# One of two expert tables read by rows: 64 tokens in slots of partitions, summed by VectorE, beside a dense product that keeps all eight PSUM banks

## The reference, cut to what matters

```python
def peer(h, wq, sub_keys, u_tab, v_tab):          # u_tab, v_tab: 16384 x 1024 float32 each
    def one(hx):
        qq = (hx @ wq).reshape(pb, PEER_HEADS, 2, PEER_HALF)
        s = jnp.einsum('nhcd,hckd->nhck', qq, sub_keys)
        s1, i1 = lax.top_k(s[:, :, 0], PEER_TOPK)
        s2, i2 = lax.top_k(s[:, :, 1], PEER_TOPK)
        cand = s1[..., :, None] + s2[..., None, :]
        top, sel = lax.top_k(cand, PEER_TOPK)
        eidx = take(i1 * PEER_NKEYS + i2, sel)      # 128 rows per token
        g = jax.nn.softmax(top, axis=-1)
        a = jax.nn.gelu(jnp.einsum('nd,nhkd->nhk', hx, u_tab[eidx]))
        return jnp.einsum('nhk,nhkd->nd', g * a, v_tab[eidx])
```

## Time and profile before

| | |
|---|---|
| median of 3 runs | 1192.62 us |
| span of the profiled execution (first to last instruction) | 1199.7 us |
| U phase ends, first value tile starts | 827.93 us |
| last value tile starts | 1193.82 us |
| TensorE busy, share of the span | 97% |
| VectorE / ScalarE / POOL busy | 71% / 53% / 52% |
| DMA over the span | 268.42 MB, 224 GB/s in the mean |

### The profile page before, as it was taken

The page is one execution under the profiler, slowest core; times in us unless marked ns, Lnnn a source line. Parts: engine busy times, 40 slices in busy tenths (PEclk is TensorE's granted clock), DMA queues, the critical chain, the costliest instruction groups (busy, mean ns, idle before and its releaser), DMA issues.

```text
span 1199.7 us, 23707 instructions
## 1 busy us (share of the span) xinstructions
PE 1165.4 (97%) x8356; PEld 1087.5 (91%) x8356; DVE 850.4 (71%) x1594; ACT 632.0 (53%) x1207; POOL 623.4 (52%) x540
## 2 busy tenths in 40 slices
PE   7999999989999999999999999999989999999998
PEld 5698989977899999999999999999879888888888
DVE  6468456654686799999958788877756556656666
ACT  6454455432353454554557776745545555555554
POOL 2422234431000287877788877031477777777770
PEclk9999899899999999999999999999999999999999
DMA  7772439767664357677676666697988888888784
GB/s 246 273 235 74 141 104 336 232 196 255 195 238 171 105 186 174 169 169 188 172 186 168 157 169 169 222 328 258 335 288 300 285 291 298 304 294 297 284 293 168
DMA packets 143079, 268.42 MB, mean 224 GB/s; under 512 B 51504, under 2 KB 81776, under 8 KB 142256
## 3 DMA queue, kind: packets, MB, share of 16 engines
q1 hardware_dynamic: 101856, 208.60, 51.3%
q0 software_dynamic: 38384, 54.89, 17.5%
q10 hardware_dynamic: 2720, 3.40, 0.8%
HBM read 250.37 MB, written 20.62 MB: 226 GB/s over the span
## 4 chain that ended last, share of the span: by engine, by line
PE 86%; issue 4%; DVE 4%; ACT 2%; DMA 2%; POOLq 1%; another core or an unknown queue 1%; POOL 0%; SPq 0%; ACTq 0%; DVEq 0%
PE ps L2285 27%; PE ps L2365 15%; PE ps L2290 13%; PE ps L2372 8%; PE ps L2409 3%; PE ps L1831 2%; PE ps L1995 2%; PE ps L2098 2%; PE ps L1851 2%; PE ps L2136 1%; PE ps L1917 1%; PE ps L2103 1%; PE ps L2339 1%; PE ps L2086 1%; PE ps L1858 1%
## 5 line engine op out<-in xcount | busy, mean ns | idle before, releaser
L1044 ACT ACTIVATE w_hi<-ring 128x1024 fp32r<-128x1024 f32 x280 | 296.6, 1059 | 320.8 <-issue 189.2
L1541 DVE TENSOR_TENSOR w_lo<-ring,w_hi 128x1024 fp32r<-128x1024 f32 x271 | 331.2, 1223 | 181.7 <-ACT w_hi L1044 86.1
L2285 PE MATMUL ps<-h_hi,w_hi 128*128 128x288 f32 x1088 | 294.5, 299 | 0.5 <-ACT w_hi L1044 0.5
L2285 PE MATMUL ps<-h_lo,w_hi 128*128 128x288 f32 x1024 | 277.0, 295 | 0.0
L628 POOL DMA_INDIRECT gates<-arena x128 | 243.2, 1900 | 64.3 <-issue 43.7
L2285 PEld LDWEIGHTS ps<-h_hi,w_hi 128*128 128x128 f32 x1088 | 205.0, 188 | 1.2 <-ACT w_hi L1044 1.0
L638 POOL DMA_INDIRECT arena<-in_v,aux x122 | 148.5, 1217 | 90.3 <-DVE aux L1715 40.0
L2285 PEld LDWEIGHTS ps<-h_lo,w_hi 128*128 128x128 f32 x1024 | 192.2, 188 | 0.0
L2290 PE MATMUL ps<-h_hi,w_lo 128*128 128x288 f32 x1088 | 167.2, 296 | 0.2 <-DVE w_lo L1541 0.2
L2365 PE MATMUL ps<-h_hi,w_hi 128*128 128x432 f32 x680 | 149.8, 361 | 3.7 <-issue 1.8
L2290 PEld LDWEIGHTS ps<-h_hi,w_lo 128*128 128x128 f32 x1088 | 151.7, 188 | 0.5 <-DVE w_lo L1541 0.5
(11 more groups left out here) (375 smaller groups left out, 2041.5 us busy)
## 6 DMA issues: line engine op xcount, KB each, us to landing
ring<-in_uT SPq DMA_DIRECT2D x128, 512.0 KB
ring<-in_v SPq DMA_DIRECT2D x128, 512.0 KB
ring<-in_wout SPq DMA_DIRECT2D x32, 512.0 KB
ring<-in_wT SPq DMA_DIRECT2D x28, 512.0 KB
gates<-aux SPq DMA_DIRECT2D x32, 256.0 KB, 5.7
act_kept<-arena SPq DMA_DIRECT2D x32, 144.0 KB
ring<-in_wtok SPq DMA_DIRECT2D x8, 512.0 KB
aux<-gates SPq DMA_DIRECT2D x16, 256.0 KB
```

Source lines behind the costliest of these rows:

```text
L1044: act.activation(w_hi[e % 2][:, :], ring[:, (W_O + e) % RING, :], ACT.Copy).then_inc(S["w_high"], 1)
L1541: dve.tensor_tensor(w_lo[e % 2][:, :], ring[:, (W_O + e) % RING, :], w_hi[e % 2][:, :].bitcast(F32), ALU.subtract)\
L2285: last = pe.matmul(ps[:, bank, 0:NT], w_hi[e % 2][:, k * P:(k + 1) * P], mov[:, k, :], start=(k == 0 and mov is mov_hi), stop=False, skip_ ...
```

## The change

The tokens by rows become 64 (two sets x of 32), the dense ones 224; the groups of `route` become 24 (the last at tile 117, it was 113).

**Slots.** The 128 partitions hold 32 tokens x 4 pairs of heads. A pair of heads has 32 experts per token, so there are 32 slots; slot i of set x is one row of 1024 columns on every partition. POOL fetches it with two requests of 128 x 512. VectorE multiplies it by a weight per partition and adds it to a sum of 128 x 1024 per set (`weigh_slot`, one `scalar_tensor_tensor` per set). At the end TensorE adds the four partitions of a token and turns the sums in one product with a 128 x 32 matrix of ones and zeros (`turn_sums`, 8 matmuls for each half of the width), straight into columns 448 to 511 of the banks that hold the dense sums. Slots stand in the program at tiles 8, 12, 15, 19, 22, ... 120: five in 18 tiles. Each slot after the second is requested when tile 10, 13, 17, ... 114 is reached and slot i - 2 has been added, since two slots per set are held.

**Width.** The two halves of the width alternate from tile to tile, in eight banks (4 to 7 and 0 to 3), so a split moving side serves two tiles. The last four tiles are ordered half 0, 0, 1, 1.

**Lists.** The row numbers are now made for slots: ScalarE copies the picked indices into place at tile 68 of the U phase (5 small copies), VectorE computes the addresses right there (`gather_lists`, before after the last group, at tile 114), and TensorE no longer turns the indices of the 32 sample tokens (12 small matmuls). `act_kept` is written with the tiles of a partition side by side.

```diff
-NE = 72
+NE = 64
+QUADS = P // NS
+SLOTS = PTOP * PH // QUADS
+HELD = 2
+def row_tile(i):
+    return 10 + (i - HELD) * 18 // 5
+def slot_tile(i):
+    return row_tile(i + 1) + 2
-VBANK = ((2, 3, 4, 5), (0, 1, 2, 3))
+VBANK = ((4, 5, 6, 7), (0, 1, 2, 3))
+V_ORDER = [(t // 2, t % 2) for t in range(PK - 4)] + [(HALF - 2, 0), (HALF - 1, 0), (HALF - 2, 1), (HALF - 1, 1)]
...
 POOL:
+            def gather_rows(x, i):
+                n = NS * x + i
+                for half in range(2):
+                    pool.indirect_dma_start(e_rows[x][i % HELD][:, half * 512:(half + 1) * 512], None,
+                                            A["v"].rearrange("t p (c f) -> (t p c) f", f=512),
+                                            bass.IndirectOffsetOnAxis(row_list[:, n:n + 1], 0), element_offset=half * 32 * P * D)\
+                        .then_inc(S[row_sems[x][i % HELD]], 16)
+            for i in range(HELD, SLOTS):
+                pool.wait_ge(S["lo_used"], E_V + row_tile(i))
+                if i > FOUR and i % FOUR == HELD:
+                    pool.wait_ge(S["s_weights"], 2 + i // FOUR)
+                for k in range(2 * (i + FOUR - HELD), 2 * (i + FOUR - HELD) + 2):
+                    if k < 2 * SLOTS:
+                        gather_value(k)
+                for x in range(2):
+                    pool.wait_ge(S["rows_used"], 2 * (i - HELD) + x + 1)
+                    gather_rows(x, i)
...
 VectorE:
             copy_lists()
+            gather_lists()
...
+            def weigh_slot(i):
+                if i % FOUR == 0:
+                    dve.wait_ge(S[f"e_in{i // FOUR % 2}"], 16 * 2 * FOUR * (i // FOUR // 2 + 1))
+                    four = lambda y: y.rearrange("p (x n) -> p x n", x=2)[:, :, i:i + FOUR]
+                    dve.tensor_tensor(four(e_weights), four(e_act), four(gT[:, ND:NT]), ALU.mult).then_inc(S["s_weights"], 1)
+                dve.wait_ge(S["s_weights"], 2 + i // FOUR + 1)
+                for x in range(2):
+                    w = e_weights[:, NS * x + i:NS * x + i + 1]
+                    dve.wait_ge(S[row_sems[x][i % HELD]], row_base[x][i % HELD] + 32 * (i // HELD + 1))
+                    if i == 0:
+                        last = dve.tensor_scalar(e_sums[x], e_rows[x][0], w, None, ALU.mult)
+                    else:
+                        dve.wait_ge(S["rows_used"], 2 * (i - 1) + x + 1)
+                        last = dve.scalar_tensor_tensor(out=e_sums[x], in0=e_rows[x][i % HELD], scalar=w, in1=e_sums[x], op0=ALU.mult, op1=ALU.add)
+                    last.then_inc(S["rows_used"], 1)
             for t in range(2, PK):
                 w_low_part(E_V + t)
-                if t + 1 < PK:
-                    mov_low_part(t + 1)
+                if t % 2 == 0 and t // 2 + 1 < HALF:
+                    mov_low_part(t // 2 + 1)
                 if PK - WEIGH_AT + t - 2 < PIECES_IN:
                     weigh_piece(PK - WEIGH_AT + t - 2)
+                if t in SLOT_AT:
+                    weigh_slot(SLOT_AT[t])
...
 TensorE:
-                if t in UNIT_TILES:
-                    weigh_unit(2 * UNIT_TILES.index(t))
-                    weigh_unit(2 * UNIT_TILES.index(t) + 1)
-                if t == PK - 2:
-                    turn_sums()
                 value_tile(t)
+                if t in (SUM_AT, SUM_AT + 1):
+                    turn_sums(t - SUM_AT)
```

More of the change, by code:

```diff
@@ L221, in low_count @@
     return e + 1 - (POOL_LOW[1] - POOL_LOW[0] if e >= POOL_LOW[1] else 0)
[L224 to L231 removed]
+V_ORDER = [(t // 2, t % 2) for t in range(PK - 4)] + [(HALF - 2, 0), (HALF - 1, 0), (HALF - 2, 1), (HALF - 1, 1)]
 def v_tile(t):
[L235 removed]
+    pp, dh = V_ORDER[t]
     return pp // 32 * 64 + dh * 32 + pp % 32
@@ L642, in gather_value @@
[L642 to L659 removed]
+            row_list, act_list = (x[:, ND:NT].bitcast(U32) for x in (i1T, i2T))
@@ L1816, in _ @@
-            dve.wait_ge(S["x1_back"], 32)
-            dve.wait_ge(S["so_turned"], 3)
-            for dh in range(2):
-                x = xT[:, 4 * dh:4 * dh + 4, ND:NT].rearrange("p k (c q) -> p k c q", q=GRP)
-                new = ps[:, 6 + dh, :].rearrange("p (k q c) -> p k c q", k=4, q=GRP)[:, :, 0:EGROUPS, :]
-                last = dve.tensor_tensor(x, x, new, ALU.add)
-            last.then_inc(S["y_ready"], 1)
+                if t in SLOT_AT:
+                    weigh_slot(SLOT_AT[t])
@@ L1823, in _ @@
+            add_sums(0, range(4))
             add_sums(1, range(4))
@@ L2355, in value_tile @@
             def value_tile(t):
-                dh = t // HALF
+                pp, dh = V_ORDER[t]
                 e = E_V + t
-                both = [mov[t % MOVES][:, 2 * h * ND:2 * h * ND + 2 * ND] for h in range(2)]
+                both = [mov[pp % MOVES][:, 2 * h * ND:2 * h * ND + 2 * ND] for h in range(2)]
                 def high(ms):
```

250 lines of the change are left out of this document (88 added, 162 removed).

## The result

The changed kernel takes 1207.16 us (median of 5 runs, 1202.27 to 1211.84) against 1193.74 (5 runs, 1190.37 to 1197.34) for the kernel before: ratio 1.0116 [1.0087, 1.0145], slower by 1.2%. The forecast was 1177, with 1158 to 1203 as its range; the time lies above it.

What follows compares the result with a forecast made beforehand. TensorE bounded the kernel before; after the change POOL's requests would, at X = 10.2: V phase 48.9 + 29.3 X = 347.8 us, 18.1 less, U phase +2.8, span 1184.4, minus 7.1 for the median: 1177 us, range 1158 to 1203.

Steps and rivals of the forecast that it cites:

- What bounds the kernel: V phase before the change: 365.9 us, 2.45 us per value tile, 17 us of waits; POOL already at its limit.
- TensorE.: V phase for TensorE alone: 36.9 us removed, 9.8 added for columns, 1.0 for turning sums; 339.8 us with waits kept.
- 4.40: Microseconds, start to start, where TensorE weighed a group of 4 tokens before; the profile after should show none.
- U phase.: Two more groups add 1.3 us, the address list moved to tile 70 adds 1.5; together +2.8 us.
- VectorE.: A sum of 128 x 1024 takes 1.28 us; a slot needs 8.1 of 9.1 us, so it fits at 89%.
- second pass: Rival: a sum takes two passes on VectorE, 2.4 us; phase 386 us, median 1215; chance 0.03.
- X: POOL's time for the six requests of a slot: 10.2 us, between bounds of 9.1 and 11.3.
- But for one only: A POOL request waits for the running VectorE operation, but for no second one, then takes some 0.82 us more.
- POOL, the term that decides: POOL's requests set the V phase: 48.9 + 29.3 X, 347.8 us at X = 10.2, 18.1 less than before.
- Its chain: Late requests make rows late; VectorE waits ahead of the sum, TensorE for the next `w_lo`, SP to reload the ring.
- The landing of 4 us: Time for requested rows to arrive, 4 us, counted after POOL's requests at the end of the V phase.
- The slower rival: POOL's requests lock to VectorE's rhythm, six taking 10.65 us or more; median 1200 to 1209 us; chance 0.20.

Runs made afterwards that it cites:

- e2: Changed kernel with the 62 sums replaced by reductions with one SBUF input, leaving out the weighted sum: 1197.31 us, 0.9979 of the kernel before.
- e4: Changed kernel with one request per row of 1024 columns instead of two of 512: 1176.22 us, 0.9821 of the kernel before.
- e10: Changed kernel with only the gates two tiles earlier: 1195.12 us, 1.0123 of the kernel before.
- a2: The changed kernel as it is, measured again beside other runs on one chip: 1204.63 us, 1.0099 of the kernel before.
- e1b: Changed kernel with the value requests made four slots earlier, run beside the unedited change: 1187.27 us, 0.9948 of the kernel before.
- e5: Changed kernel with one request per row of 1024 columns and values requested four slots earlier: 1167.22 us, 0.9855 of the kernel before.
- e3: Changed kernel with values requested four slots earlier and reductions in place of the sums: 1183.35 us, 0.9879 of the kernel before.

## Why the prediction was wrong

By its own steps:

- *What bounds the kernel*: TensorE's tiles took 2.45 us and POOL ran near its limit; no run contradicts it.
- *TensorE.* A tile takes 2.51 us for 2.53. The turns lengthen two tiles to 4.23 and 4.32, together by 3.5 us where 1.8 was in the sum: each turn has 16 small matmuls (four blocks of columns for each of two sets), not 8 as the section on the change and the sum have it, and they take 1.72 us. No 4.40 is left.
- *U phase.* +2.8 (420.9 to 423.7), as forecast, with the gap at tile 70 where it was expected (the tile takes 2.2 us more, behind `w_lo`, for 1.5).
- *VectorE.* 1282 ns for 1.28 us; no second pass. `w_lo` is unchanged.
- *X, the time of six requests*: 10.14 us in the first trace, 9.7 on chip C, for 10.2. The mechanism (a sum holds a request) is shown by e2. "But for one only" is wrong: of 184 requests 87 were free, 88 waited for one operation, two for two (2.0 us), six for three (3.70 us each) and one for seven (6.64 us); before, 108 of 208 were free and 100 waited for one. Against a wait of one operation (some 1.4 us) the nine longer ones add about 20 us to the 184 requests, an estimate from these lengths, or 0.6 to X. That 10.2 was hit is so in part luck.
- **The step that failed is the phase's formula in "POOL, the term that decides"**: "28 slots x X and two with 4 requests instead of 6, i.e. 29.3 X". It holds only if POOL never stands still from tile 10 to the last slot. With the measured X it gives 48.9 + 29.3 x 10.14 = 346.0 us, the trace has 377.7. Of the missing 31.7 us, 23.6 are time in which POOL stands idle between its first gated request and its last (the 9.9 us at tile 10 come before that, inside the formula's 27 us, of which 26.2 were used). The other part is the end: behind POOL's last request the trace has 30.8 us, the formula 21.9. The last two slots have four requests each, POOL is ahead of the tiles again and waits 3.6 us for its last gate, and the rest is TensorE's own tiles. On chip C the terms are 25.6, 29.3 x 9.68, 34.0 of idle time and 30.7, together 373.9 as measured.

Why POOL idles is what the prediction didn't see. Its chain knew one wait of VectorE, for rows. The other stands in the diff: `weigh_slot` waits at every fourth slot for the values of four slots, and the last of these is asked for in the block of the slot after: behind the slot's own four row requests, and behind a gate that lies two tiles, 5 us, ahead of the use. Two requests take 2.2 us at least, and from the end of the second to VectorE's product lie 2.7 to 4.7 us in the seven later groups. So the gate leaves no margin: in e4, where POOL waits for 107 us at its gates, the values still cost VectorE 15.3 us. In the change itself it is mostly POOL that is late: in five of the seven groups it comes to these two requests with hardly a pause (0.30 to 0.40 us), and a gate two tiles earlier helps the values nothing (e10). VectorE then waits, `w_lo` behind it, TensorE behind `w_lo`, and POOL at its gate behind TensorE: a loop in which a late value stops its own supplier. Seven times, about 31 us of the phase with the slow tiles behind them; asking earlier gave 20.3 of them back (a2 to e1b), since the waits for rows then grow. The landing of 4 us was in the sum once, at the end of the phase, where it belonged at each place at which the requests and the landing are longer than the look-ahead.

The slower rival, at 1200 to 1209 us, has the right time for the wrong reason: it wanted X over 10.65 (by its own formula the old phase is reached at 10.72). The granted clock's 11 us were in no rival; the prediction has no term for slow tiles, and the profile of before showed 1.00 from 860 to 1180 us.

DMA and ScalarE did as expected: 275 GB/s, lower since the phase is longer and moves 4 MB less, and no wait for `w_hi` that counts.

## What to carry to other kernels

For each wait that a change adds, put three numbers side by side before any rate: when the last thing waited for is asked for (with the gate ahead of it), how long its requests and its landing take, and when it is used; a batch of four is as late as its fourth. Ask as well what stands ahead of that request in its engine's list: an earlier gate is worth nothing to a request whose engine comes to it late. A sum by the rate of one engine holds only while that engine never waits, so look for the loop by which a late result holds up whoever produces it. Where requests cost the same for any width, halving their number did more than any reordering tried here: wide rows with early values take 1167 us where the kernel before takes 1182.

## What the runs showed of the hardware

- A request on POOL can be held over several VectorE operations that follow each other without a gap: 6.64 us over seven of them in the changed kernel, 8.91 us over nine in e5, each ending 0.82 us after the end of one. Most are released at the first end, with the next operation starting at once all the same; the held ones of 3.70 us all started within 0.02 us of a `w_lo` and had `w_lo`, `w_lo`, split ahead of them. What decides isn't settled. Where no such sums run the requests stay at 2.0 us or less (both traces of the kernel before, e2), but for one of 3.5 in e3. One of the six, VectorE:

```profile
907.92 2.35 DVE L1522 TENSOR_TENSOR w_lo<-ring,w_hi 128x1024 fp32r<-128x1024 f32 x2
910.19 0.61 DVE L1747 TENSOR_TENSOR mov<-arena,mov 128x448 fp32r<-128x448 f32 x1
911.38 1.23 DVE L1522 TENSOR_TENSOR w_lo<-ring,w_hi 128x1024 fp32r<-128x1024 f32 x1 [0.57 <-ACT w_hi L1025]
```

  and POOL:

```profile
906.20 1.43 POOL L659 DMA_INDIRECT arena<-in_v,aux  x1 [0.30 <-issue]
907.93 3.70 POOL L659 DMA_INDIRECT arena<-in_v,aux  x1 [0.30 <-issue]
911.94 1.49 POOL L668 DMA_INDIRECT arena<-act_kept,aux  x1 [0.31 <-issue]
```

- Seven stalls of 2.7 to 4.8 us cost TensorE 0.7 to 2.1 us more each in the tile behind them, 1.6 in the mean, through the granted clock (0.50 in the rows above).
- A `scalar_tensor_tensor` with two f32 inputs in SBUF takes 1282 ns for 1024 columns, a `tensor_tensor` 1222: the half throughput that the Trainium skill (Vector Engine (DVE) Microarchitecture Reference, the points that are easy to get wrong) gives for this form isn't there.
